# Sixteen pairs of experts behind a transformer block: where the first expert weights are kept, and when the first slot selections are made

## The chip, the cores and the metric

The kernel runs on one core of a Trainium2 chip. The metric is device time in microseconds; three runs of the kernel before took 969.98, 970.21 and 971.9 us, median 970.21. One more execution, the profiled one, took 969.27 us, and its trace spans 967.1 us.

## The reference, cut to what matters

The program computes two blocks over 256 tokens of width 1024, all in float32. The first block is a norm, a recurrence (RG-LRU), sliding-window attention, a feed-forward part and a gated embedding. The second block is latent attention, pooled mixing, cross-attention over a memory of 256 tokens and then a mixture of 32 experts, of which each token takes two. The change concerns the last part:

```python
def hierarchical_moe(xn, w_rg, b_rg, w_re, b_re, w_gate, w_up, w_down):
    ...
    for e in range(N_EXPERTS):
        hid = jax.nn.silu(xn @ w_gate[e]) * (xn @ w_up[e])
        out = out + (hid * cw[..., e:e + 1]) @ w_down[e]
    return out
```

and the memory's cross-attention just before it, `softmax(q k^T) v @ w_o`. An expert has 1024x256 gate and up matrices and a 256x1024 down matrix, so the weights of all 32 experts are about 100 MB, each read once.

## The kernel before, in words

**Units.** All weights come in units of one slot of 128 partitions x 2048 float32 (1 MB), in an order fixed by `plan_units` and numbered i. The dense units, 0 to NUD-1, end with four of w_xo (the output matrix of the memory's attention) and the small router unit. They go to four `raw` slots in turn (NRAW = 4). ScalarE and VectorE split each into a high and a low part (`wh`, `wl`, three pairs, NW = 3; lines 998 and 1548), and TensorE does three products per tile on the parts (lines 472 to 474).

**Experts.** After NUD come 96 expert units for 16 pairs of experts. Pair p has four `moe_in` units (gate and up, two DMAs of 512 KB each) and two `moe_out` units (down, one DMA of 1 MB); `moe_out` of pair p-1 stands behind `moe_in` of pair p. They are not split: TensorE multiplies from the slot itself. They use 15 slots in a ring, `MSLOTS`. So the first 15 units are loaded as soon as their places come free from earlier work, and each later unit is a refill, loaded when the unit 15 places ahead of it has been used (`used`). Refill 1 is the unit numbered 15 after the first, counting from 0, and goes where unit 0 was.

**The queue.** `load(i)` waits on SP for a semaphore and issues the unit's DMAs (line 416). All weight loads are on SP, in program order, so one that waits holds back all behind it. Before the change the ring is `ga, gb, bt`, three raw slots, the six `wh`/`wl` buffers, `s0`, a raw slot, `s1`. The first three units are issued among the w_xo units; the others need a late split or the last uses of `wh` and `wl`.

**The sparse part.** `pe_sparse` (called when no expert has more than 48 tokens) gathers the tokens of eight experts at a time into `XG` (line 2451), and goes through the pairs: `pe_rise(p)` is gate and up (line 2480), then `pe_down(p-1)` (line 2503), then `pe_choose(p+1)`, `pe_turn_hidden(p)`, `pe_spread(p-2)`. `pe_choose(p)` (line 2430) makes the pair's selection and slot weights in a bank of PSUM, which ScalarE copies to `SET` (`act_choose`, line 2568) and VectorE reduces to `CS` (`dve_slot_weights`, line 2634). Its bank is `rise_bank(max(p, 1))`, so selections 0 and 1 both use the bank in which pair 1 rises, and pair p's rise cannot start before both readers are done. Between rise and down the activation is ScalarE's tanh and two VectorE operations on `HS` (lines 2592, 2645, 2648), a transpose on TensorE (`pe_turn_hidden`, line 2488) and a copy to `HT` (line 2608). For pair 0 there is no down of an earlier pair between rise and transpose.

Work buffers `RA`, `RB`, `RC`, `RD`, `KT` belong to attention, recurrence and memory. They and `th`, `tl` are given back before the sparse part, whose own buffers (`XN`, `SEL0`, `XG`, `YY` and others) take the place.

Of the kernel before, what the change touches and what calls it, by code (L numbers as in the profile page):

```python
# [74 lines left out]
def plan_units():  # L75
# [63 lines left out]
    [f"raw_{i}" for i in (*range(NRAW), "ga", "gb", "bt", "s0", "s1", *(f"{x}{n}" for n in range(NW) for x in ("wh", "wl")))] +  # L139
# [21 lines left out]
def build(nc, A, out):  # L161
    with ExitStack() as ctx:
# [24 lines left out]
        BT = sb("BT", 2304)  # L187
        WH = [sbe(f"wh{i}", SLOT, R) for i in range(NW)]
        WL = [sbe(f"wl{i}", SLOT, R) for i in range(NW)]
        RA = sbe("RA", 2080)  # L190
        RB = sbe("RB", 2048)
        RC = sbe("RC", 2048)
        RD = sbe("RD", 1024)
        KT = sbe("KT", 1024)
        TH, TL = [0, 0], [0, 0]
        for i in range(2):
            TH[i], TL[i] = sbe(f"th{i}", 2048, R), sbe(f"tl{i}", 2048, R)
# [32 lines left out]
        FLAT.update({"ga": GA[:, :], "gb": GB[:, :], "bt": BT[:, 0:2048], "s0": S0[:, :], "s1": S1[:, :]})  # L230
        last_w = [i % NW for i in range(NUD - 1 - NW, NUD - 1)]
        MSLOTS = ["ga", "gb", "bt"] + late_slots[:-1] + [f"{x}{n}" for n in last_w for x in ("wh", "wl")] + ["s0"] + late_slots[-1:] + ["s1"]
# [142 lines left out]
        def load(i):  # L375
            _, parts = units[i]
            kc, w = shape_of(i)
            flat = FLAT[slot(i)]
            dst = v3(flat, kc, w)
            m = i - NUD  # L380
            if m >= NM:
                SP.wait_ge(S["used"], i - NM + 1)
            elif m >= NM - 2:
                SP.wait_ge(S["used"], ROUTER + 1)
            elif m == NM - 3:
                SP.wait_ge(S["square"], SQ["w_xo_2"] + 4)
            elif m >= 2 + NRAW:
                SP.wait_ge(S["used"], ROUTER - NW + (m - 2 - NRAW) // 2 + 1)
            elif m in (0, 1, 2):
                SP.wait_ge(S["turn_mm"], TB_["m2"] + 8)  # L390
            elif i >= NRAW:
                before = NUD - NRAW + m - 3 if m >= 3 else i - NRAW
                if before == 0:
                    SP.wait_ge(S["used"], 1)
                else:
                    SP.wait_ge(S["lo"], before)
# [25 lines left out]
        def sp_main():  # L422
# [26 lines left out]
            for i in range(NUD + 3, NUD + NM):  # L449
                load(i)  # L450
# [285 lines left out]
        def pe_main():  # L736
# [233 lines left out]
            for t in range(2):  # L970
                m = PE.matmul(PB[b1][:, 36 * t:36 * t + 36], KT[0:100, 128 * t:128 * t + 128], cst("fold", 36)[0:100, :], start=(t == 0),
# [182 lines left out]
        def act_main():  # L1154
# [353 lines left out]
            ACTE.activation(KT[0:100, 0:256], PB[banks_of(("router", 0))[0]][0:100, 0:256], ACT.Copy).then_inc(S["logits"], 1)  # L1508
# [13 lines left out]
        def pool_main():  # L1522
# [6 lines left out]
            POOL.wait_ge(S["xs_mm"], 4)  # L1529
            POOL.wait_ge(S["xv_mm"], 4)  # L1530
# [856 lines left out]
        def sparse(late):  # L2387
# [68 lines left out]
            def pe_rise(p):  # L2456
# [4 lines left out]
                for r in range(4):  # L2461
# [71 lines left out]
            def pe_sparse():  # L2533
# [10 lines left out]
                for p in range(NP + 1):  # L2544
# [4 lines left out]
                    if p + 1 < NP:  # L2549
# [8 lines left out]
                    if p == 0:  # L2558
                        pe_turn_hidden(0)
# [18 lines left out]
            def act_sparse():  # L2578
# [7 lines left out]
                act_choose(0)  # L2586
                for p in range(NP + 1):
                    if p < NP:
# [13 lines left out]
                    if p + 1 < NP:  # L2602
# [33 lines left out]
            def dve_sparse():  # L2636
                dve_split_weights()
                dve_slot_weights(0)
                for p in range(NP + 1):
# [14 lines left out]
                    if p + 1 < NP:  # L2654
# [206 lines left out]
        FLAT.update({f"{x}{n}": sb(f"m{x}{n}", SLOT)[:, :] for x in ("wh", "wl") for n in range(NW)})  # L2861
# [41 lines left out]
```

## Time and profile before

| | |
|---|---|
| median of three runs | 970.21 us |
| profiled execution | 969.27 us |
| its span | 967.1 us |
| TensorE busy | 951.4 us, 98% |
| VectorE, ScalarE busy | 534.3 us, 469.7 us |
| first gather to last expert matmul | about 724 to 956 us |
| granted TensorE clock, mean | 0.997 |

How to read it: matmuls are pipelined and their ends are modelled, so that two in a row overlap by a little, and the start of the next row tells the pace. A row of the timeline that merges several instructions gives the start of the first and the time over all. A DMA row gives the median time from issue on SP to landing; asked for a narrow stretch it is that of one DMA. Idle time in brackets is that of the engine just before the row, with what ended it.

### The profile page before, as it was taken

The page shows a single profiled execution, that of the slowest core. Times are in us where ns is not written, and L with a number is a line of the kernel's source. Part 1 is how long each engine was busy: PE and PEld are TensorE (multiplying, and loading weights), DVE is VectorE, ACT ScalarE, POOL GpSimd, SP SyncE. Part 2 cuts the span into 40 slices and gives each one's busy share as a digit, 9 for nine tenths or more (in the row PEclk, how much of TensorE's full clock was granted, in tenths as well). Part 3 has the DMA queues.
Part 4 walks back from the last instruction along what each step waited for, and adds up shares of the span by engine and source line. Part 5 has one row for each costly group of instructions (what it writes and reads, how often), then busy time and mean ns, then how long its engine had stood idle before and what let it go on. Part 6 is the DMA issues. An engine that isn't in the chain of part 4 may idle for free.

```text
span 967.1 us, 13220 instructions
## 1 busy us (share of the span) xinstructions
PE 951.4 (98%) x5313; PEld 723.6 (75%) x5313; DVE 534.3 (55%) x848; ACT 469.7 (49%) x733; POOL 2.5 (0%) x12
## 2 busy tenths in 40 slices
PE   9999999999999999999999999999999999999996
PEld 8879887887889889989889887889874354544442
DVE  5888896675666555554586875676453212122123
ACT  5588655756444444444566756445452131211213
POOL 0000000000000000000000000000000000000000
PEclk9999999999999999999999999999999999999998
DMA  9935565424456545554645735365389999999994
GB/s 319 305 132 175 174 218 175 168 94 175 144 183 198 194 175 175 175 179 153 204 146 178 237 113 168 137 238 198 93 323 379 396 393 394 394 393 394 393 394 168
DMA packets 107265, 223.48 MB, mean 231 GB/s; under 512 B 10185, under 2 KB 15042, under 8 KB 107202
## 3 DMA queue, kind: packets, MB, share of 16 engines
q1 hardware_dynamic: 104752, 219.10, 63.7%
q10 hardware_dynamic: 2450, 3.51, 1.1%
q8 instruction: 44, 0.72, 0.3%
q14 instruction: 19, 0.16, 0.0%
HBM read 221.54 MB, written 1.05 MB: 230 GB/s over the span
## 4 chain that ended last, share of the span: by engine, by line
PE 96%; DVE 2%; ACT 1%; issue 1%; DMA 1%; ACTq 0%; DVEq 0%
PE pb L472 21%; PE pb L474 21%; PE pb L473 21%; PE pb L2480 12%; PE pb L2503 6%; PE pb L2518 3%; PE pb L2451 2%; PE pb L562 2%; PE pb L633 1%; PE pb L645 1%; PE pb L582 1%; PE pb L709 1%; PE pb L732 1%; PE pb L536 1%; PE pb L2430 1%
## 5 line engine op out<-in xcount | busy, mean ns | idle before, releaser
L1548 DVE TENSOR_TENSOR wl<-raw,wh 128x2048 fp32r<-128x2048 f32 (+3 forms) x112 | 246.4, 2208 | 96.6 <-ACT wh L998 96.4
L998 ACT ACTIVATE wh<-raw 128x2048 fp32r<-128x2048 f32 (+3 forms) x112 | 206.1, 1847 | 111.5 <-PE pb L474 102.2
L472 PE MATMUL pb<-wh,th 128*128 128x512 f32 (+2 forms) x620 | 247.8, 400 | 0.0
L474 PE MATMUL pb<-wh,tl 128*128 128x512 f32 (+2 forms) x620 | 241.5, 390 | 0.0
L473 PE MATMUL pb<-wl,th 128*128 128x512 f32 (+2 forms) x620 | 241.3, 389 | 0.0
L472 PE MATMUL pb<-th,wh 128*128 128x256 f32 x528 | 152.0, 288 | 0.0
L474 PE MATMUL pb<-th,wl 128*128 128x256 f32 x528 | 149.0, 282 | 0.0
L473 PE MATMUL pb<-tl,wh 128*128 128x256 f32 x528 | 148.7, 282 | 0.0
L472 PEld LDWEIGHTS pb<-wh,th 128*128 128x128 f32 x620 | 116.7, 188 | 27.0 <-issue 4.1
L474 PEld LDWEIGHTS pb<-wh,tl 128*128 128x128 f32 x620 | 116.7, 188 | 25.4
L473 PEld LDWEIGHTS pb<-wl,th 128*128 128x128 f32 x620 | 116.9, 189 | 22.6
L472 PEld LDWEIGHTS pb<-th,wh 128*128 128x128 f32 x528 | 99.6, 189 | 3.2 <-issue 2.7
L473 PEld LDWEIGHTS pb<-tl,wh 128*128 128x128 f32 x528 | 99.6, 189 | 0.5
L474 PEld LDWEIGHTS pb<-th,wl 128*128 128x128 f32 x528 | 99.4, 188 | 0.0
L2645 DVE SCALAR_TENSOR_TENSOR HS<-HS,pb 128x256 f32<-128x256 f32 x16 | 6.7, 422 | 141.5 <-ACT HS L2592 141.5
L2592 ACT ACTIVATE HS<-pb 128x256 f32<-128x256 f32 x16 | 6.1, 384 | 120.9 <-PE pb L2480 120.9
L2653 DVE TENSOR_TENSOR YL<-pb,YH 128x512 fp32r<-128x512 f32 x32 | 22.1, 692 | 34.7 <-ACT YH L2601 34.7
L2601 ACT ACTIVATE YH<-pb 128x512 fp32r<-128x512 f32 x32 | 19.1, 597 | 39.6 <-PE pb L2503 39.6
L2480 PE MATMUL pb<-raw,XG 128*64 128x512 f32 x152 | 35.2, 596 | 0.0
L1014 ACT ACTIVATE th<-pb,PC 128x256 fp32r<-128x256 f32 x45 | 18.8, 479 | 27.3 <-PE pb L562 27.3
L2480 PEld LDWEIGHTS pb<-raw,XG 128*64 128x64 f32 x152 | 10.7, 137 | 20.0 <-issue 20.0
L2518 PE MATMUL pb<-YH,SET 128*128 128x512 f32 x60 | 24.9, 415 | 0.0
(396 smaller groups left out, 1071.3 us busy)
## 6 DMA issues: line engine op xcount, KB each, us to landing
raw<-in_w_in SPq DMA_DIRECT2D x31, 1024.0 KB, 5.1
raw<-in_w_up SPq DMA_DIRECT2D x16, 1024.0 KB, 5.6
raw<-in_w_down SPq DMA_DIRECT2D x16, 1024.0 KB, 4.8
raw<-in_w_exp_gate SPq DMA_DIRECT2D x19, 512.0 KB, 11.8
raw<-in_w_exp_up SPq DMA_DIRECT2D x19, 512.0 KB, 11.7
raw<-in_w_xkv SPq DMA_DIRECT2D x8, 1024.0 KB, 5.0
raw<-in_w_exp_down SPq DMA_DIRECT2D x8, 1024.0 KB, 13.9
mwh<-in_w_exp_gate SPq DMA_DIRECT2D x12, 512.0 KB, 11.7
```

The costliest lines, as they stand in the source:

```text
L472: PE.matmul(o, lh, rh, start=start, stop=False, skip_group_check=True)
L473: PE.matmul(o, lh, rl, start=False, stop=False, skip_group_check=True)
L474: return PE.matmul(o, ll, rh, start=False, stop=stop, skip_group_check=True)
L562: m = PE.transpose(PB[b][:, 128 * t:128 * t + 128], x, ident)
L998: ACTE.activation(hi_of(i), raw_of(i), ACT.Copy).then_inc(S["hi"], 1)
L1548: DVE.tensor_tensor(lo_of(i), raw_of(i), hi_of(i).bitcast(F), ALU.subtract).then_inc(S["lo"], 1)
L2451: m = PE.matmul(b[:, 0:384].rearrange("p (e n) -> p e n", e=SET_E), XN4[i][:, t, k], slots_of(SEL0, t), start=(t == 0 and i == 0), stop=(t ...
L2480: m = PE.matmul(b[64 * j:64 * j + 64, :].rearrange("p (g n) -> p g n", g=2), XG[:, c + CAP * j:c + CAP * j + 64], w[:, :, j, k], start=(kk ...
L2503: m = PE.matmul(PB[6 + h][64 * j:64 * j + 64, :], HT[p % 2][:, 128 * k + 64 * j:128 * k + 64 * j + 64], w[:, j, 512 * h:512 * h + 512], st ...
L2518: m = PE.matmul(PB[2 * t + h][:, :], SET[p % 4][:, 128 * t:128 * t + 128], YY[p % 2][i][:, 512 * h:512 * h + 512], start=(p == 0 and i == ...
L2601: ACTE.activation(YY[(p - 1) % 2][0][:, 512 * h:512 * h + 512], PB[6 + h][:, :], ACT.Copy).then_inc(S["yy_hi"], 1)
L2653: DVE.tensor_tensor(lo, PB[6 + h][:, :], hi.bitcast(F), ALU.subtract).then_inc(S["yy_lo"], 1)
```

## The change

The ring still has 15 slots, but other ones. `RA`, `RB`, `RC` and the joined `RD` and `KT` (`RDK`) are now permanent and serve as slots, `th0` and `tl0` too, and the six `wh`/`wl` buffers no longer do; the sparse part's buffers lie in their place. Each slot has a wait of its own. The router's copy goes to `ROW` instead of `KT`, and the clearing of `SEL0` waits for the last w_xo unit. In the sparse part, selections 1 and 2 move into the rises of pairs 0 and 1, ahead of their fourth unit, and the transpose of pair 0 moves behind the first unit of pair 1.

```diff
-        MSLOTS = ["ga", "gb", "bt"] + late_slots[:-1] + [f"{x}{n}" for n in last_w for x in ("wh", "wl")] + ["s0"] + late_slots[-1:] + ["s1"]
+        MSLOTS = ["rd", "ga", "gb", "bt", late_slots[0], "th", "tl", "ra", "rc", late_slots[1], "rb", late_slots[2], "s0", late_slots[3], "s1"]
...
             if m >= NM:
                 SP.wait_ge(S["used"], i - NM + 1)
-            elif m >= NM - 2:
+            elif m >= 0 and slot(i) == "rd":
+                SP.wait_ge(S["used"], U["gates2", 3, 1] + 1)
+            elif m >= 0 and slot(i) in ("ga", "gb", "bt"):
+                SP.wait_ge(S["turn_mm"], TB_["m2"] + 8)
+            elif m >= 0 and slot(i) in ("th", "tl"):
+                SP.wait_ge(S["used"], U["w_xq_2", 1, 1] + 1)
+            elif m >= 0 and slot(i) in ("ra", "rc"):
+                SP.wait_ge(S["xs_mm"], 4)
+            elif m >= 0 and slot(i) == "rb":
+                SP.wait_ge(S["xv_mm"], 4)
+            elif m >= 0 and slot(i) == "s0":
+                SP.wait_ge(S["square"], SQ["w_xo_2"] + 4)
+            elif m >= 0 and slot(i) in ("s1", late_slots[3]):
                 SP.wait_ge(S["used"], ROUTER + 1)
...
                 if i == U["w_xo_2", 0, 0]:
-                    for m in range(3):
+                    for m in range(4):
                         load(NUD + m)
...
-            POOL.wait_ge(S["xs_mm"], 4)
-            POOL.wait_ge(S["xv_mm"], 4)
+            POOL.wait_ge(S["used"], ROUTER)
             POOL.memset(SEL0[:, :].bitcast(F).rearrange("p (a n) -> p a n", n=64)[:, :, CAP:64], 0.0).then_inc(S["zero"], 1)
...
                     elif p == 0 and r == 2:
                         pe_choose(0)
+                    elif p == 1 and r == 1:
+                        pe_turn_hidden(0)
+                    if p < 2 and r == 3:
+                        pe_choose(p + 1)
...
-                    if p + 1 < NP:
+                    if 2 <= p < NP - 1:
                         pe_choose(p + 1)
...
-                    if p == 0:
-                        pe_turn_hidden(0)
```

`act_sparse` and `dve_sparse` take the copies and reductions of selections 1 and 2 in the same new order.

On TensorE, from the third unit of pair 0 to the first unit of pair 2. `IW,SEL` is a selection, `XG` a rise, `CT,HS` a transpose, `HT` a down. Before:

```order
L2480 MATMUL pb<-BT,XG 64x512 x4
L2480 MATMUL pb<-raw,XG 64x512 x4
L2430 MATMUL pb<-IW,SEL 128x256 x2
L2488 MATMUL pb<-CT,HS 128x128 x2
L2480 MATMUL pb<-raw,XG 64x512 x8
L2480 MATMUL pb<-mwh,XG 64x512 x4
L2480 MATMUL pb<-mwl,XG 64x512 x4
L2503 MATMUL pb<-mwh,HT 64x512 x4
L2503 MATMUL pb<-mwl,HT 64x512 x4
L2430 MATMUL pb<-IW,SEL 128x256 x2
L2488 MATMUL pb<-CT,HS 128x128 x2
L2480 MATMUL pb<-mwh,XG 64x512 x4
```

And the same place in the changed kernel:

```order
L2488 MATMUL pb<-GB,XG 64x512 x4
L2434 MATMUL pb<-IW,SEL 128x256 x2
L2488 MATMUL pb<-BT,XG 64x512 x4
L2488 MATMUL pb<-raw,XG 64x512 x4
L2496 MATMUL pb<-CT,HS 128x128 x2
L2488 MATMUL pb<-mth,XG 64x512 x4
L2488 MATMUL pb<-mtl,XG 64x512 x4
L2434 MATMUL pb<-IW,SEL 128x256 x2
L2488 MATMUL pb<-RA,XG 64x512 x4
L2511 MATMUL pb<-RC,HT 64x512 x4
L2511 MATMUL pb<-raw,HT 64x512 x4
L2496 MATMUL pb<-CT,HS 128x128 x2
```

A unit of rise now stands between each selection and the rise that needs its bank, and one between the end of pair 0's rise and its transpose. Nothing is added or dropped. The next row in the changed kernel is the first unit of pair 2.

On SP, the loads behind the router's. Before, from the third of the three raw slots on:

```order
L416 DMA raw<-in_w_exp_gate 128x2x512
L416 DMA raw<-in_w_exp_up 128x2x512
L416 DMA mwh<-in_w_exp_gate 128x2x512
L416 DMA mwh<-in_w_exp_up 128x2x512
L416 DMA mwl<-in_w_exp_gate 128x2x512
L416 DMA mwl<-in_w_exp_up 128x2x512
L416 DMA mwh<-in_w_exp_down 128x2x1024
L416 DMA mwl<-in_w_exp_down 128x2x1024
```

Now, from the router's on:

```order
L421 DMA raw<-in_w_router_expert 128x8x32
L421 DMA raw<-in_w_exp_gate 128x2x512
L421 DMA raw<-in_w_exp_up 128x2x512
L421 DMA mth<-in_w_exp_gate 128x2x512
L421 DMA mth<-in_w_exp_up 128x2x512
L421 DMA mtl<-in_w_exp_gate 128x2x512
L421 DMA mtl<-in_w_exp_up 128x2x512
L421 DMA RA<-in_w_exp_gate 128x2x512
L421 DMA RA<-in_w_exp_up 128x2x512
L421 DMA RC<-in_w_exp_down 128x2x1024
L421 DMA raw<-in_w_exp_down 128x2x1024
```

Two units of operand space (`mth`, `mtl` are `th0`, `tl0`) and two of attention's work space now stand between the first raw slot and the second, where the six split buffers (`mwh`, `mwl`) stood behind the third. `RB` follows the last row shown.

## Rows read from the trace of the kernel before

**Rows 1.** Page, parts 1 and 2: busy time by engine, GB/s in 40 slices.

```profile
PE 951.4 (98%) x5313; PEld 723.6 (75%) x5313; DVE 534.3 (55%) x848; ACT 469.7 (49%) x733; POOL 2.5 (0%) x12
...
GB/s 319 305 132 175 174 218 175 168 94 175 144 183 198 194 175 175 175 179 153 204 146 178 237 113 168 137 238 198 93 323 379 396 393 394 394 393 394 393 394 168
```

**Rows 2.** TensorE's waits from 700 us on: in total, times, longest us.

```profile
PE pb L2480 <- ACT SET L2568: 1.2, 1, 1.2
PE pb L2488 <- DVE HS L2648: 1.0, 1, 1.0
```

**Rows 3.** Timeline of TensorE: start, us, line, tiles, count, idle before.

```profile
738.16 0.50 PE L2430 MATMUL pb<-IW,SEL 128*128 128x256 f32 x2
739.69 0.44 PE L2488 MATMUL pb<-CT,HS 128*128 128x128 f32 x2 [1.02 <-DVE HS L2648]
740.14 3.65 PE L2480 MATMUL pb<-raw,XG 128*64 128x512 f32 x16
...
752.48 1.94 PE L2480 MATMUL pb<-mwh,XG 128*64 128x512 f32 x8 [1.17 <-ACT SET L2568]
...
925.04 1.94 PE L2480 MATMUL pb<-mwl,XG 128*64 128x512 f32 x8
...
938.01 1.94 PE L2480 MATMUL pb<-raw,XG 128*64 128x512 f32 x8
```

**Rows 4.** Timeline of SP's issues, the last first loads and some refills.

```profile
720.92 1.23 SPq L416 DMA_DIRECT2D S<-in_w_exp_down  x1
730.08 0.37 SPq L416 DMA_DIRECT2D GA<-in_w_exp_down  x1
...
734.67 0.47 SPq L416 DMA_DIRECT2D GB<-in_w_exp_up  x1
...
745.54 0.37 SPq L416 DMA_DIRECT2D mwh<-in_w_exp_down  x1
...
932.67 3.74 SPq L416 DMA_DIRECT2D raw<-in_w_exp_down  x3
```

**Rows 5.** DMA issues in narrow stretches (720, 730, 735, 745, 932 us): KB, us to landing.

```profile
S<-in_w_exp_down SPq DMA_DIRECT2D x1, 1024.0 KB, 14.0
...
GA<-in_w_exp_down SPq DMA_DIRECT2D x1, 1024.0 KB, 7.4
...
GB<-in_w_exp_up SPq DMA_DIRECT2D x1, 512.0 KB, 5.5
...
mwh<-in_w_exp_down SPq DMA_DIRECT2D x1, 1024.0 KB, 8.9
...
raw<-in_w_exp_down SPq DMA_DIRECT2D x1, 1024.0 KB, 13.9
```

**Rows 6.** Timeline of the weight loads on TensorE, the last wait for a DMA.

```profile
946.58 0.21 PEld L2503 LDWEIGHTS pb<-raw,HT 128*64 128x64 f32 x4 [0.65 <-DMA raw<-in_w_exp_down]
```

**Rows 7.** DMA issues on an idle queue: w_xkv, page part 6; a pair at 693.8 us.

```profile
raw<-in_w_xkv SPq DMA_DIRECT2D x8, 1024.0 KB, 5.0
...
raw<-in_w_exp_up SPq DMA_DIRECT2D x1, 512.0 KB, 4.9
```

**Rows 8.** Stretches: length, busy PE, PEld, DVE, ACT, POOL, PEclk, DMA share, GB/s.

```profile
740.00:750.00 10.00, 9.98 (x48) 4.03 (x48) 0.90 (x2) 0.93 (x3) 0.00 (x0) 1.00 1.02 373
760.00:780.00 20.00, 20.00 (x96) 9.83 (x93) 6.04 (x14) 4.51 (x11) 0.00 (x0) 1.00 1.04 393
```

**Rows 9.** Timeline of ScalarE and VectorE around the first selection and activation.

```profile
734.69 0.38 ACT L2568 ACTIVATE SET<-pb 128x256 fp32r<-128x256 f32 x1 [1.72 <-PE pb L2430]
735.10 0.35 DVE L2634 TENSOR_REDUCE CS<-pb 64x1 f32<-64x2 f32 x2 [3.05 <-ACT SET L2568]
738.28 0.38 ACT L2592 ACTIVATE HS<-pb 128x256 f32<-128x256 f32 x1 [3.21 <-PE pb L2480]
```

**Rows 10.** The w_xo loads: SP's issues, one's landing (651 to 653 us), a split on ScalarE.

```profile
652.27 10.35 SPq L416 DMA_DIRECT2D raw<-in_w_xo  x3
...
raw<-in_w_xo SPq DMA_DIRECT2D x1, 1024.0 KB, 8.0
...
671.48 1.91 ACT L998 ACTIVATE wh<-raw 128x2048 fp32r<-128x2048 f32 x1
```

More of the change, by code:

```diff
@@ L138 @@
 SEMAPHORES = (
-    [f"raw_{i}" for i in (*range(NRAW), "ga", "gb", "bt", "s0", "s1", *(f"{x}{n}" for n in range(NW) for x in ("wh", "wl")))] +
+    [f"raw_{i}" for i in (*range(NRAW), "rd", "ga", "gb", "bt", "th", "tl", "ra", "rc", "rb", "s0", "s1")] +
     ["d_x", "d_rows", "d_first", "d_const", "d_bd", "d_bcast", "d_mem", "d_mem1", "d_pos", "d_gffn", "d_poolw", "d_p", "d_fing",
@@ L187, in build @@
         BT = sb("BT", 2304)
+        RA = sb("RA", 2080)
+        RB = sb("RB", 2048)
+        RC = sb("RC", 2048)
+        RDK = sb("RDK", 2048)
+        RD, KT = RDK[:, 0:1024], RDK[:, 1024:2048]
+        TH, TL = [sbe("th0", 2048, R), 0], [sbe("tl0", 2048, R), 0]
         WH = [sbe(f"wh{i}", SLOT, R) for i in range(NW)]
         WL = [sbe(f"wl{i}", SLOT, R) for i in range(NW)]
[L190 to L197, printed above, removed]
+        TH[1], TL[1] = sbe("th1", 2048, R), sbe("tl1", 2048, R)
         BD = BT[:, 0:1024]
@@ L229, in build @@
         FLAT = {n: RAW[n][:, :] for n in range(NRAW)}
-        FLAT.update({"ga": GA[:, :], "gb": GB[:, :], "bt": BT[:, 0:2048], "s0": S0[:, :], "s1": S1[:, :]})
-        last_w = [i % NW for i in range(NUD - 1 - NW, NUD - 1)]
-        MSLOTS = ["ga", "gb", "bt"] + late_slots[:-1] + [f"{x}{n}" for n in last_w for x in ("wh", "wl")] + ["s0"] + late_slots[-1:] + ["s1"]
+        FLAT.update({"rd": RDK[:, :], "ga": GA[:, :], "gb": GB[:, :], "bt": BT[:, 0:2048], "ra": RA[:, 0:2048], "rc": RC[:, :], "rb": RB[:, :], "s0": S0[:, :], "s1": S1[:, :]})
+        MSLOTS = ["rd", "ga", "gb", "bt", late_slots[0], "th", "tl", "ra", "rc", late_slots[1], "rb", late_slots[2], "s0", late_slots[3], "s1"]
         NM = len(MSLOTS)
@@ L382, in load @@
                 SP.wait_ge(S["used"], i - NM + 1)
-            elif m >= NM - 2:
-                SP.wait_ge(S["used"], ROUTER + 1)
[L385 to L390, printed above, removed]
+            elif m >= 0 and slot(i) == "rd":
[11 more added lines that the diff above has]
+            elif m >= 0 and slot(i) in ("s1", late_slots[3]):
+                SP.wait_ge(S["used"], ROUTER + 1)
+            elif m >= 0:
+                SP.wait_ge(S["lo"], NUD - NRAW + late_slots.index(slot(i)))
             elif i >= NRAW:
-                before = NUD - NRAW + m - 3 if m >= 3 else i - NRAW
-                if before == 0:
+                if i == NRAW:
                     SP.wait_ge(S["used"], 1)
                 else:
-                    SP.wait_ge(S["lo"], before)
+                    SP.wait_ge(S["lo"], i - NRAW)
             for (name, lead, r0, n, c0, cw, at) in parts:
@@ L446, in sp_main @@
                 if i == U["w_xo_2", 0, 0]:
-                    for m in range(3):
+                    for m in range(4):
                         load(NUD + m)
-            for i in range(NUD + 3, NUD + NM):
+            for i in range(NUD + 4, NUD + NM):
                 load(i)
@@ L970, in pe_main @@
             for t in range(2):
-                m = PE.matmul(PB[b1][:, 36 * t:36 * t + 36], KT[0:100, 128 * t:128 * t + 128], cst("fold", 36)[0:100, :], start=(t == 0),
+                m = PE.matmul(PB[b1][:, 36 * t:36 * t + 36], ROW[0:100, 128 * t:128 * t + 128], cst("fold", 36)[0:100, :], start=(t == 0),
                               stop=True, skip_group_check=True)
@@ L1507, in act_main @@
             act_done(("router", 0), 0)
-            ACTE.activation(KT[0:100, 0:256], PB[banks_of(("router", 0))[0]][0:100, 0:256], ACT.Copy).then_inc(S["logits"], 1)
+            ACTE.activation(ROW[0:100, 0:256], PB[banks_of(("router", 0))[0]][0:100, 0:256], ACT.Copy).then_inc(S["logits"], 1)
             ACTE.activation(unused, eps, ACT.Exp).then_inc(S["root"], 1)
@@ L2586, in act_sparse @@
                 act_choose(0)
+                act_choose(1)
                 for p in range(NP + 1):
+                    if p == 1:
+                        act_choose(2)
                     if p < NP:
@@ L2860, in build @@
         early.close()
-        FLAT.update({f"{x}{n}": sb(f"m{x}{n}", SLOT)[:, :] for x in ("wh", "wl") for n in range(NW)})
+        FLAT.update({"th": sb("mth", 2048)[:, :], "tl": sb("mtl", 2048)[:, :]})
         normed = ExitStack()
```

7 lines of the change are left out of this document (5 added, 2 removed).

## Prediction

> **What bounds the kernel now.** I read four views in this order. The page first: TensorE is busy 951.4 of 967.1 us, and from the thirtieth slice on (a slice is 24.2 us) the DMA queues move 379 to 396 GB/s without a pause [rows 1]. So in the experts' part two resources look full at once. The question is which of them ends the kernel.
>
> TensorE's waits come second. From 700 us on, two waits of more than half a microsecond stand in the list, 1.2 us for the copy of a selection and 1.0 us for the activation of pair 0 [rows 2], both at the start, before pair 2 [rows 3]. After that TensorE goes at a fixed pace: pair 14 begins at 925.04 us and pair 15 at 938.01, so 12.97 us for a pair's six units, 2.16 us a unit [rows 3].
>
> The DMA side comes third, from issues and landings. Refill 1 is issued at 730.08 us and lands 7.4 us later, at 737.5. Refill 2 lands at 734.67 + 5.5 = 740.2, refill 7 at 745.54 + 8.9 = 754.4, and refill 79 at 932.67 + 13.9 = 946.6 [rows 4, 5]. Between refills 2 and 7 that is 14.2 / 5 = 2.85 us a unit, between 7 and 79 it is 192.2 / 72 = 2.67 us a unit, which is 1.049 MB at 393 GB/s [rows 8].
>
> So TensorE is the faster of the two by half a microsecond a unit. It lives on the 15 units loaded ahead, and the lead is used up just at the end: at 946.58 us TensorE waits 0.65 us for refill 79, the second down unit of pair 14, the only wait for a DMA in this part [rows 6]. The balance is nearly exact. A gain on TensorE alone is eaten by that wait, and the end then follows the landing of refill 79.
>
> **The change part by part.** I cost each part against the profiled execution, 969.27 us, which is 0.94 us below the median of 970.21 us. The difference that comes out is put on the median.
>
> *The transposes behind the first unit of pair 1, selection 1 in the rise.* Before, selection 1 starts at 738.16 us, the transpose waits until 739.69 and pair 1 begins at 740.14 [rows 3]. A selection followed by a rise takes about 0.43 us, so pair 1 could have begun at 738.6, 1.55 us sooner. The transposes come back between its first two units and take the 0.45 us that they took. The net is 1.1 us, about the 1.0 us that the list of waits has. The cover is one unit of rise, 3.65 / 2 = 1.8 us or 1.72 us of pace. It must hide two things. First, selection 0 to its last reader: copy from 734.69, reductions to 735.10 + 0.35 = 735.45, against a selection that started at about 734.15, so 1.3 us; it fits. Second, tanh to transpose: 738.28 to 739.69 is 1.4 us [rows 3, 9], plus some 0.2 us before the tanh; it fits by 0.1 us. If it does not fit, the loss is that tenth or two.
>
> *Selection 2 in the rise of pair 1.* It takes away the 1.17 us before 752.48 [rows 3]. It now waits for `HT` of pair 0, which is ready two units earlier. Both together give TensorE 2.2 us, or 2.3 by the timeline.
>
> *TensorE's bound.* If no DMA held it, the end would come earlier by 2.2 us and by the 0.65 us wait of rows 6, that is 2.9 us.
>
> *First loads earlier.* There are 15 slots before and after. Before, the last first load is issued at 720.92 us and lands at 734.9 [rows 4, 5], so when refill 1 is issued at 730.08, earlier units still land for another 4.8 us. After, four units are issued among the w_xo units, `th` and `tl` when the last w_xq unit is used, `RA` and `RC` after the memory's scores, `RB` after its values; only the last three (`s0`, a raw slot, `s1`) wait for the end of w_xo or the router. I expect all to have landed by about 724 us, and the queue to be idle until 730. It is not asked for anything then: a refill needs a used unit, and the first unit is used at 730.08 as before, because the gathers and the router ahead of it do not depend on these loads. That is the main point. What the early loads can win is only what stands in front of the refills at 730, not their five or ten units.
>
> *Where the refills land.* Refill 1 then takes the 5.0 us of a unit alone and lands at 735.1. Refill 2 is a pair of DMAs; alone, the second lands 4.9 us after its issue [rows 7], so at 734.67 + 4.9 = 739.6, against 740.2. The head start of 2.4 us at refill 1 has shrunk to 0.6 us at refill 2, since between the two stand the gathers, and nothing can be loaded while they run. From refill 2 on, units are asked for faster than they land. At 2.67 us a unit refill 7 lands at 752.9, 1.5 us earlier than before; at 2.85, the pace that these very refills had, it lands at 753.8, 0.6 us earlier. The ends are 0.6 and 1.5. Nothing excludes that a queue with nothing ahead does a little worse still, so I put the lower end at zero. I take 0.6, since the same units in the same order at nearly the same times are the nearest row. From refill 7 on the pace is 2.67 in both kernels.
>
> A page of the Trainium skill prices this otherwise: DMA: Bandwidth & Descriptors, section Anatomy of one DMA, gives about 2.0 us plus bytes over 436 GB/s for one DMA, on its software path. By an estimate from that page refill 2's second DMA would land 3.2 us after its issue, at 737.9, and the gain would be 2.3 us instead of 0.6. The rows have 4.9 us for such a DMA on an idle queue, so the measurement decides and the sum does not use it.
>
> *The end.* TensorE reaches refill 79 at 946.0 - 2.2 = 943.7 us; it lands at 946.6 - 0.6 = 946.0. TensorE waits there 2.3 us or so, and everything behind follows 0.6 us earlier than before.
>
> *At nothing.* The fourth unit among the w_xo loads is 2.7 us more in front of the second w_xo unit, issued at 652.27 us and landed 8.0 us later, at 660.3. The splits have other units to do first: that unit's is not before 671.48 [rows 10], so 8 us are left to cover it. One unit more on SP costs it under 1 us of issuing, long before anything waits. The clearing of `SEL0` moves to the end of w_xo, some 18 us ahead of selection 0, its only reader that waits for it. The router's copy has the same size in another buffer. The sparse part's buffers in the split weights' place are written after the router, when the last split pair is used.
>
> The sum: 0.6 us less, 968.7 us for an execution like the profiled one and **969.6 us** for the median.
>
> **The rivals.**
>
> *A: the tail of loads doesn't bind, TensorE's gain counts in full.* For it: the wait in the list before is only 0.65 us, the idle queue at 724 to 730 us may serve the first refills better than I take, and fewer loads beside the router may help a little. Against: refill 79 would have to land 2.9 us earlier, which no pace seen gives, even 2.67 us from refill 2 on gives 1.5. It gives 970.2 - 2.9 = 967.3 us. The Trainium skill, on the same page in its section Rules for kernel authors, says to issue a DMA early and wait on it late; taken by itself that speaks for A, and the trace limits it by the time at which refills can be issued.
>
> *B: slower, by shallow refills.* The queue starts at 730 us with nothing in it and not, as before, with up to 4.8 us of work. In the first stretch of refills it moved 373 GB/s against 393 later [rows 8]. If refills go at 2.85 us until the queue is deep, and depth takes longer to build because nothing stood ahead, each such unit costs 0.18 us. It starts with 1.5 us to spend, so it decides beyond 8 units, and is a measurable loss beyond (1.5 + 1.9) / 0.18 = 19 units. With 30 it costs 3.9 us, so 974 us. Against it: the queue gains 0.5 us of depth a unit from TensorE's faster pace, and refill 7 already waits 8.9 us.
>
> *C: the new selections wait.* If ScalarE's or VectorE's readers of selection 0 or 1 are late by more than the unit that covers them, TensorE stops where it did not. The price is under 1 us, and the refills' landing still sets the end: 970.2 us, no change.
>
> **How the numbers follow.** A difference of 0.2%, 1.9 us, is about what a measurement of this kernel can tell from no change. My forecast, an end set by the refills and 0 to 1.5 us earlier, has 0.78. A has 0.11, B 0.08, C 0.03. A is the only case that is faster by over 1.9 us, B the only one that is slower. So faster is 0.11, same 0.81, slower 0.08. The range: the forecast's own ends are 968.7 and 970.2, the runs shown lie up to 1.7 us above their median, and the lower end reaches to A. That is 967.3 to 971.2.
>
> **What would show it.** Right: the two waits of rows 2 gone; pair 2 begins at about 750.2 us instead of 752.48; the queue without bytes between about 724 and 731 us; refill 1 landing at 735, refill 2 at 739.6, and refill 79 within 1.5 us of 946.0; TensorE waiting 2 us or more in total for `in_w_exp_down` or its neighbours near the end. It would be wrong if pair 0's first unit were used much before or after 730.08 us, if the DMA rate between 760 and 940 us were other than 393 GB/s, or if TensorE showed a new wait in the dense part between 640 and 714 us. A shows in refill 79 landing before 944 us, B in refill 7 landing after 755 us and the queue below 380 GB/s beyond 780 us.

## Result and profile after

| | before | after |
|---|---|---|
| median of the runs, us | 970.67 (969.98 to 971.9, 4 runs) | 964.57 (963.91 to 964.85, 4 runs) |
| ratio | 1 | 0.9935, interval 0.9918 to 0.9952 |
| profiled execution, us; its span | 969.27; 967.1 | 964.85; 963.0 |

(The row of before has a fourth run, 971.13 us, beside the three of the section on the metric.) The change makes the kernel 6.1 us faster where 0.6 was forecast, and 964.57 us lies below the range of 967.3 to 971.2. The profiled execution of before is shorter than all four of its runs, that of after is the longest of its four, so the two profiles show 4.4 of the 6.1.

The page of the changed kernel, busy time and bytes:

```profile
PE 947.5 (98%) x5313; PEld 722.7 (75%) x5313; DVE 534.4 (55%) x848; ACT 470.1 (49%) x733; POOL 2.5 (0%) x12
...
GB/s 314 303 143 173 155 238 179 156 107 163 152 189 190 204 175 175 175 181 156 202 150 175 246 104 175 131 259 223 290 205 286 393 394 393 394 393 395 393 396 157
```

Against [rows 1] TensorE does the same 5313 instructions in 3.9 us less, and slices 32 to 39, the steady refills, have the same rate as before, 393 to 396 GB/s. So the gain is TensorE's own time, and it isn't in the refills. The timeline of TensorE, the changed kernel (start, us, line, tiles, count):

```profile
723.61 1.94 PE L2488 MATMUL pb<-RDK,XG 128*64 128x512 f32 x8
...
731.95 0.50 PE L2434 MATMUL pb<-IW,SEL 128*128 128x256 f32 x2
...
734.15 1.89 PE L2488 MATMUL pb<-raw,XG 128*64 128x512 f32 x8
735.97 0.44 PE L2496 MATMUL pb<-CT,HS 128*128 128x128 f32 x2
...
746.02 1.94 PE L2488 MATMUL pb<-RB,XG 128*64 128x512 f32 x8
```

and the same first unit before:

```profile
728.10 1.94 PE L2480 MATMUL pb<-GA,XG 128*64 128x512 f32 x8
```

The first expert unit starts at 723.61 instead of 728.10 us, 4.5 us earlier. Pair 2 starts 22.4 us behind it, where it was 24.4, so TensorE does gain its 2.0 us in the first pairs. But from the first expert unit to the end of the span it is 963.0 - 723.6 = 239.4 us, and before 967.1 - 728.1 = 239.0: the experts' part, where all that was meant happens, gained nothing. TensorE's waits and the weight loads that waited, changed kernel:

```profile
PE pb L2511 <- DMA GB<-in_w_exp_down: 0.6, 1, 0.6
PE pb L2511 <- DMA BT<-in_w_exp_down: 0.6, 1, 0.6
...
PE pb L2488 <- DMA GA<-in_w_exp_up: 0.3, 1, 0.3
```

```profile
937.38 0.20 PEld L2488 LDWEIGHTS pb<-GA,XG 128*64 128x64 f32 x4 [1.22 <-DMA GA<-in_w_exp_up]
939.94 0.20 PEld L2511 LDWEIGHTS pb<-GB,HT 128*64 128x64 f32 x4 [1.50 <-DMA GB<-in_w_exp_down]
942.50 0.20 PEld L2511 LDWEIGHTS pb<-BT,HT 128*64 128x64 f32 x4 [1.50 <-DMA BT<-in_w_exp_down]
```

The two waits of [rows 2] are gone and three waits for refills stand near the end, as forecast. The list puts them at 1.5 us in total. The starts tell more: the three units above start 2.56 us apart each, where a unit's pace is 1.72.

So the 4.5 us come from the dense part, where the same work is done in the same order. Weights that are loaded on the way show how they grow: the w_attn_proj unit is issued 0.1 us earlier than before, w_mix_out 3.1 and w_xo 4.0 us. SP's issues, after and then before:

```profile
203.26 0.37 SPq L421 DMA_DIRECT2D raw<-in_w_attn_proj  x1
...
590.21 0.37 SPq L421 DMA_DIRECT2D raw<-in_w_mix_out  x1
...
639.68 0.37 SPq L421 DMA_DIRECT2D raw<-in_w_xo  x1
```

```profile
203.36 0.37 SPq L416 DMA_DIRECT2D raw<-in_w_attn_proj  x1
...
593.34 0.37 SPq L416 DMA_DIRECT2D raw<-in_w_mix_out  x1
...
643.64 0.37 SPq L416 DMA_DIRECT2D raw<-in_w_xo  x1
```

None of TensorE's waits in the dense part went; its products follow each other more closely. In one run of products over split weights, fifteen in a row without a gap, after and then before:

```profile
616.68 0.39 PE L477 MATMUL pb<-wh,th 128*128 128x512 f32 x1
...
619.85 0.39 PE L479 MATMUL pb<-wh,tl 128*128 128x512 f32 x1
```

```profile
619.67 0.39 PE L472 MATMUL pb<-wh,th 128*128 128x512 f32 x1
...
622.92 0.39 PE L474 MATMUL pb<-wh,tl 128*128 128x512 f32 x1
```

Fourteen steps take 3.17 us after, 0.226 a product, and 3.25 before, 0.232. There are 3 x 576 products of this width. Grouped by line and form (busy us, mean ns of one), after and then before:

```profile
L478 PE MATMUL pb<-wl,th 128*128 128x512 f32 x576 | 224.7, 390 | 0.0
...
L478 PE MATMUL pb<-tl,wh 128*128 128x256 f32 x528 | 149.4, 283 | 0.0
```

```profile
L473 PE MATMUL pb<-wl,th 128*128 128x512 f32 x576 | 227.1, 394 | 0.0
...
L473 PE MATMUL pb<-tl,wh 128*128 128x256 f32 x528 | 148.7, 282 | 0.0
```

A product is shown from its start to its modelled end and overlaps the next, so I compare the **pace**: the mean step from one start to the next in a run of products, over the whole trace. With 512 columns, where the split weights move through the array, it is 232.5 ns before and 227.9 after. With 256, where the operands `th` and `tl` move, it is 120.4 and 121.2. That is 1728 x 4.6 = 7.9 us less and 1584 x 0.8 = 1.3 us more. Of these 6.6 us some are lost and 4.5 arrive. A part of the loss can be seen: the weight loads of the first of the three products wait longer for VectorE's part of the split, `wl`. In us and times, before (line 472) and then after (line 477):

```profile
  DVE wl L1548: 0.4, 2
```

```profile
  DVE wl L1552: 2.2, 6
```

The products, their data and their clock are the same: the granted clock of the profiled execution is 0.998 after, and 0.997 to 0.998 in the kernels below. What differs is where the buffers lie. Counted from the program's allocations, in bytes of a partition, with the rest over 256 in brackets:

| | before | after |
|---|---|---|
| `wh0`, `wl0`, ... | 112672 (32), 137248 (32) | 161952 (160), 186528 (160) |
| `th0` | 194720 (160) | 145568 (160) |
| `th1` | 211104 (160) | 211104 (160) |

Of the work buffers only `RA` isn't a multiple of 256 bytes long; its 8320 bytes are 128 more. Before, it lies between the split weights (`wh`, `wl`) and the operands (`th`, `tl`), after, ahead of both. So the distance from the split weights to the operands, over 256, was 128 and is 0. "Distance" below means this rest, split weights minus operands. The count puts the first buffer, `raw0`, at 16512 bytes, which no view shows. The distances don't depend on it; the places themselves, of the slots too, do.

### The profile page after: what moved, and what is told of

Same layout as the page of the kernel before. It is cut to its first block, busy times and chain, and to the rows that moved or that the text cites. A ratio compares the mean times of both kernels' runs of the same rounds, so it can differ in the third digit from the quotient of the medians.

```text
span 963.0 us, 13218 instructions
## 1 busy us (share of the span) xinstructions
PE 947.5 (98%) x5313; PEld 722.7 (75%) x5313; DVE 534.4 (55%) x848; ACT 470.1 (49%) x733; POOL 2.5 (0%) x12
## 3 DMA queue, kind: packets, MB, share of 16 engines
HBM read 221.54 MB, written 1.05 MB: 231 GB/s over the span
## 4 chain that ended last, share of the span: by engine, by line
PE 83%; DVE 7%; ACT 4%; issue 3%; DMA 2%; SPq 1%; POOL 0%; ACTq 0%; DVEq 0%; POOLq 0%
PE pb L477 17%; PE pb L479 17%; PE pb L478 17%; PE pb L2488 11%; PE pb L2511 5%; PE pb L2526 3%; PE pb L2455 2%; DVE wl L1552 2%; ACT wh L1003 2%; PE pb L567 2%; DMA BT<-in_w_exp_down 1%; PE pb L638 1%; DMA raw<-in_w_in 1%; PE pb L650 1%; PE pb L714 1%
## 5 line engine op out<-in xcount | busy, mean ns | idle before, releaser
L479 PE MATMUL pb<-wh,tl 128*128 128x512 f32 (+2 forms) x620 | 239.0, 385 | 0.0
L478 PE MATMUL pb<-wl,th 128*128 128x512 f32 (+2 forms) x620 | 238.8, 385 | 0.0
## 6 DMA issues: line engine op xcount, KB each, us to landing
raw<-in_w_exp_gate SPq DMA_DIRECT2D x18, 512.0 KB, 11.2
S<-in_w_exp_down SPq DMA_DIRECT2D x6, 1024.0 KB, 13.5
```

The lines of the kernel that those rows point to most:

```text
L478: PE.matmul(o, lh, rl, start=False, stop=False, skip_group_check=True)
L479: return PE.matmul(o, ll, rh, start=False, stop=stop, skip_group_check=True)
```

## Experiments

**First round: parts of the change.** The theory: the gain is the places of the buffers, by the distance of 128 or 0. The rivals: the early loads bring it (fewer transfers beside the last dense products), or the selections do.

*e1*, the kernel before with one buffer elsewhere: loads, ring and selections stay.

```diff
+        RA = sbe("RA", 2080)
         WH = [sbe(f"wh{i}", SLOT, R) for i in range(NW)]
         WL = [sbe(f"wl{i}", SLOT, R) for i in range(NW)]
-        RA = sbe("RA", 2080)
...
+        XNLP = sb("XNL", 2080, R)
...
-        XN = [sbe("XNH", 2048, R, normed), sbe("XNL", 2048, R, normed)]
+        XN = [sbe("XNH", 2048, R, normed), XNLP[:, 0:2048]]
```

(`XNLP` has `RA`'s size and stands in the place that it leaves, so that the sparse part still fits.)

> The kernel before, with nothing moved but the work buffer RA, which now lies ahead of the six split buffers wh and wl instead of behind them. So their addresses in a partition are a multiple of 256 bytes plus 160, as in the changed kernel, instead of plus 32; the operands th and tl stay where they were, order of work and loads too. Theory 1, the dense part got faster because of where the split buffers lie relative to a 256-byte boundary: the 512-column products start every 227 ns instead of 230 to 232, the first gather comes about 4.5 us earlier, and the time is 4 to 6 us lower (965 us). Theory 2, it is the region (the far end of the partition, or the distance to th and tl): no change, within 1 us of before. Theory 3, it is the loads or another part of the change: no change either.

*e2*, the kernel before with the new order of selections and of the first transpose alone:

> The kernel before, with only the new order of the first selections and of pair 0's transpose; ring of slots, loads and addresses as before. My forecast's working: TensorE saves 2.2 us before pair 2, the refills land as before (refill 1 at 737.5 us, refill 7 a few tenths earlier), refill 79 is waited for 2 to 3 us, and the time is 0 to 0.5 us lower. If the tail of loads did not bind: 2.2 to 2.9 us lower. The pace of the dense part stays at 230 to 232 ns.

*e3*, the changed kernel with the distance put back to 128 and nothing else (a column is 4 bytes):

```diff
+        sbe("PADA", 32)
         WH = [sbe(f"wh{i}", SLOT, R) for i in range(NW)]
         WL = [sbe(f"wl{i}", SLOT, R) for i in range(NW)]
+        sbe("PADB", 32)
         TH[1], TL[1] = sbe("th1", 2048, R), sbe("tl1", 2048, R)
```

> The changed kernel, with 128 unused bytes ahead of the split buffers and 128 more ahead of th1, so that wh and wl lie at a multiple of 256 bytes plus 32 again, in the far region, and all th and tl at plus 160. Theory 1 (place relative to a 256-byte boundary): 512-column products at 230 to 232 ns again, the time 4 to 6 us above the changed kernel, 969 to 970.5 us. Theory 2 (region or distance): still 227 ns and 964.6 us. Theory 3 (loads or another part): still 964.6 us.

*e4*, the changed kernel with the order of selections of before (the hunks of `pe_sparse`, `act_choose` and `dve_slot_weights` undone):

> The changed kernel, with the first selections and pair 0's transpose put back to the old order; new ring, loads and addresses stay. Theory 1 and 2: the dense part keeps its 227 ns, so 964.6 us plus what the selections are worth. By my working of the end (refills decide) that is 0 to 0.5 us, as TensorE's own 2.2 us only lengthen its waits near the end: 964.6 to 965.1 us. If TensorE decides: 966.8 us.

Measured, with the start of the first expert unit in the profiled execution:

| kernel | us, median (range, runs) | ratio | pace 512, 256 | first expert unit |
|---|---|---|---|---|
| e1 | 965.16 (964.86 to 965.93, 5) | 0.994, 0.9927 to 0.9953 | 227.9, 121.3 | 723.99 |
| e2 | 971.22 (970.41 to 972.71, 11) | 1.0005, 0.9996 to 1.0013 | 232.4, 120.4 | 728.94 |
| e3 | 971.01 (969.51 to 971.81, 11) | 0.9999, 0.999 to 1.0008 | 232.4, 120.4 | 728.50 |
| e4 | 964.74 (963.85 to 966.91, 6) | 0.9941, 0.9929 to 0.9954 | 227.8, 121.2 | 722.49 |

This settles it from both sides. One buffer moved (and `XNL` put in the place it left) gives the kernel before the whole gain (e1), and 256 bytes of padding take it all from the changed kernel, whose early loads and new selections remain (e3). Both rivals fall. The start of the first expert unit says the same. One execution differs from the next, but the two groups stay apart: 728.10 to 728.94 us in the four profiles with distance 128 (before, e2, e3, e5), 722.49 to 724.42 in the eight with distance 0 (the changed kernel, e1, e4, and e7, e10, e11, c1, c2 below).

The selections are worth nothing (e2 against before, e4 against the changed kernel). TensorE's waits say why. In e4 both of [rows 2] are back; in e2, where they are gone, refills are waited for instead:

```profile
PE pb L2484 <- ACT SET L2572: 1.2, 1, 1.2
PE pb L2492 <- DVE HS L2652: 1.0, 1, 1.0
```

```profile
PE pb L2484 <- DMA GB<-in_w_exp_up: 0.8, 1, 0.8
PE pb L2507 <- DMA BT<-in_w_exp_down: 0.6, 1, 0.6
PE pb L2507 <- DMA raw<-in_w_exp_down: 0.6, 1, 0.6
```

1.2 + 1.0 us against 0.8 + 0.6 + 0.6: forecast step by step, and confirmed. What the early loads give is read from kernels that differ in nothing else but the places, at the same distance and with the same selections: e1 and e4, 965.16 and 964.74, or e2 and e3, 971.22 and 971.01. That is 0.4 and 0.2 us, less than the intervals can tell from nothing.

**Second round: distance or place.** If the distance decides, moving everything alike changes nothing.

*e5*, the kernel before, `sb("PADA", 32)` ahead of `WH`: split weights at 160, operands at 32, distance 128 as before.

> The kernel before, with 128 unused bytes ahead of wh0, so that everything behind moves up: wh and wl now lie at a multiple of 256 bytes plus 160, and th and tl at plus 32 (before: 32 and 160). Theory 1a, what counts is that wh and wl have the same place as th and tl relative to 256 bytes (160 and 160 in the changed kernel): here they are 128 apart as before, so 230 to 232 ns and 971 us. Theory 1b, what counts is the place of wh and wl alone, or of the moving operand (wh and wl in the 512-column products): 227 ns and 965 us for the 512-column products; the 256-column ones, whose moving operand is th, may change with th.

*e10*, the changed kernel, `sb("PADA", 32)` ahead of `th0`: all at 32, distance 0.

> The changed kernel, with 128 unused bytes ahead of th0: wh, wl, th and tl all lie at a multiple of 256 bytes plus 32. Theory 1a (same place): 227 ns and 964.6 us, as the changed kernel. Theory 1b (plus 160 for wh and wl itself is what is fast): 232 ns and 970 to 971 us.

*e7*, the same with `sb("PADA", 24)`: all at 0.

> The changed kernel, with 96 unused bytes ahead of th0: wh, wl, th and tl all at a multiple of 256 bytes. Theory 1a: 227 ns, 964.6 us. Theory 1b leaves it open. If starting on a boundary is worth something in itself, the 256-column products fall below 120 ns and the time below 964 us.

*e11*, the changed kernel with 256 bytes where e3 has 128 (`PADA` and `PADB` of 64 columns): distance 0 over 256, another one over 512.

> The changed kernel, with 256 unused bytes ahead of wh0 and 256 more ahead of th1: all of wh, wl, th and tl keep plus 160 relative to 256 bytes, but wh and wl lie 256 bytes off th and tl relative to 512 and to any larger power of two up to 2048. If 256 bytes are the measure: 227 ns and 964.6 us, as the changed kernel. If it is a larger one (512, 1024 or 2048): 232 ns and 970 to 971 us.

*e8* and *e9*, the changed kernel with `PADA`, `PADB` of 24 and 40, and of 16 and 48 columns: distance 96 and 64.

> The changed kernel, with 96 unused bytes ahead of wh0 and 160 ahead of th1: wh and wl at a multiple of 256 bytes, th and tl at plus 160, so 96 apart (160 the other way round). Theory 1a in its strict form: any distance other than 0 is slow, 232 ns and 970 to 971 us. If only a distance of 128 is slow: 227 ns and 964.6 us. Something between would speak for a dependence by degrees.

> The changed kernel, with 64 unused bytes ahead of wh0 and 192 ahead of th1: wh and wl at a multiple of 256 bytes plus 224, th and tl at plus 160, so 64 apart. Theory 1a in its strict form (any distance within 256 bytes is slow, as 96 and 128 were): 232 ns and 970 to 971 us. If only the place within 64 bytes counts: 227 ns and 964.6 us.

*c1* and *c2* are the changed kernel and e7 once more, as controls.

> The changed kernel once more, beside the kernel at plus 0, to compare them on one chip. All theories: 964.6 us, 227 ns.

> The kernel with wh, wl, th and tl at a multiple of 256 bytes once more. It had 963.2 us with the same 227 ns as the changed kernel at 964.6. If that difference is real: 1 to 1.5 us below the changed kernel again. If it was the chip or chance: within 0.5 us of it.

**Third round: other distances, and the slots.** *e15* (48 and 16 columns) has distance 192, *e16* (8 and 56) has 32.

> The changed kernel with wh and wl at a multiple of 256 bytes plus 96, th and tl at plus 160, so wh lies 192 above or 64 below th. If the pace goes by how far apart the two are, in either direction: as 64 apart, 116.8 and 229.5 ns, 962 to 963 us. If it goes by the direction too: other paces, up to the 120 and 232.5 ns of 128 apart with 971 us.

> The changed kernel with wh and wl at plus 192, th and tl at plus 160, so 32 apart. Distances 0, 64, 96, 128 had 227.9, 229.5, 233.4, 232.5 ns for the 512-column products and 121.2, 116.8, 119.6, 120.4 for the 256-column ones. If the pace changes smoothly between 0 and 64: 228 to 229 and 118 to 119 ns, about 963.5 us. If being 32 off a multiple of 64 costs by itself (as 96 seems to): 232 ns or more, 968 to 971 us.

| distance | kernels | pace 512, 256 | by the two paces, us | us, median (range, runs) | first expert unit |
|---|---|---|---|---|---|
| 128 | e5 | 232.5, 120.6 | +0.3 | 971.02 (969.62 to 972.19, 11) | 728.40 |
| 0 | e10 | 227.9, 121.3 | -6.5 | 965.03 (964.55 to 966.44, 5) | 724.42 |
| 0 | e11 | 227.8, 121.2 | -6.9 | 964.67 (964.24 to 965.83, 5) | 722.85 |
| 0 | c1 | 227.9, 121.2 | -6.7 | 964.69 (963.71 to 964.91, 5) | 722.92 |
| 0 | e7 | 227.9, 121.3 | -6.5 | 963.22 (962.87 to 963.73, 5) | 722.68 |
| 0 | c2 | 227.9, 121.2 | -6.7 | 963.21 (962.24 to 963.61, 5) | 723.05 |
| 64 | e9 | 229.5, 116.8 | -10.9 | 962.34 (960.25 to 962.77, 5) | 719.72 |
| 96 | e8 | 233.4, 119.6 | +0.3 | 970.26 (969.73 to 971.81, 11) | 728.28 |
| 192 | e15 | 233.3, 119.2 | -0.5 | 969.95 (969.08 to 971.89, 11) | 728.06 |
| 32 | e16 | 233.2, 119.7 | +0.1 | 970.18 (969.63 to 971.16, 11; one more took 2057.25) | 728.86 |

The fourth column is 1728 times the step of the one pace from before plus 1584 times that of the other. It parts the kernels into the same three groups as the first expert unit (near 728, 723 and 720 us), though not in the same order within a group. Of the saving in that column between 57% (e10) and 83% (e7) arrive there. The distance decides, not the place (e5, e10), and at distance 0 another 256 bytes change nothing (e11). It is not symmetric: 64 above is the best, 192, which is 64 below, is as bad as 128. The two widths don't agree on the best distance either. I had expected one smooth rule or one favoured place; both fell, and no cause inside TensorE or SBUF is shown here. ScalarE and VectorE write the next splits while TensorE multiplies, and no run takes them out, so it isn't shown either that TensorE's two reads alone make the difference.

In e9 the first expert unit starts 3.2 us earlier than in the changed kernel beside it (c1), but the median is only 2.35 us lower: TensorE waits for refills four times near the end, 2.4 us in the list, where c1 has three waits and 2.0:

```profile
PE pb L2490 <- DMA GA<-in_w_exp_up: 0.8, 1, 0.8
PE pb L2513 <- DMA GB<-in_w_exp_down: 0.6, 1, 0.6
PE pb L2513 <- DMA BT<-in_w_exp_down: 0.6, 1, 0.6
...
PE pb L2513 <- DMA S<-in_w_exp_down: 0.4, 1, 0.4
```

**The slots.** e7 and c2 beat c1 by 1.5 us at the same pace, and their gain stands behind the first expert unit (238.4 us from there to the end of the span in both; in the other kernels above it is 239.3 to 240.7, and before 239.0). Their DMA rate is 397 GB/s. Stretch 760 to 930 us, the changed kernel and then e7:

```profile
760.00:930.00 170.00, 170.00 (x808) 78.45 (x805) 31.34 (x74) 39.10 (x83) 0.00 (x0) 1.00 1.04 394
```

```profile
760.00:930.00 170.00, 170.00 (x807) 78.90 (x803) 32.16 (x76) 39.51 (x84) 0.00 (x0) 1.00 1.04 397
```

In e7 two of the 15 slots, `th0` and `tl0`, begin on a multiple of 256 bytes. The question was whether 64 bytes would do. (By the count of places above, 6 slots of the changed kernel and 8 of e7 lie on 64 bytes, not 8 and 10 as the expectation of e13 has it; the test is the same.) *e13* puts every slot on a multiple of 64 (`sb("PADG", 8)` ahead of `GA`); *e14* is e13 with distance 64 (and `PADA` 16, `PADB` 48).

> The changed kernel, with 32 unused bytes ahead of GA. Everything behind moves up by 32 bytes: wh, wl, th and tl stay at the same place relative to each other (all plus 192), and all 15 slots of the expert ring now start on a multiple of 64 bytes, where 8 of 15 did in the changed kernel and 10 of 15 in the kernel with the operands at plus 0. Theory S, the transfers are faster into slots on 64 bytes (397 GB/s between 760 and 930 us with 10 of 15, 394 with 8): about 405 GB/s with all 15, a pace of 227 ns as before, the experts' part shorter by 2 to 4 us until TensorE decides, so 961 to 963 us. Theory T, the 397 GB/s came from something else in that kernel (starting at a multiple of 256): 394 GB/s and 964.6 us.

> The same, with 64 more unused bytes ahead of wh0 and 192 ahead of th1: slots on 64 bytes, and wh and wl 64 bytes off th and tl, as in the run that had 962.3 us. Theory S: both gains add, about 116.8 ns for the 256-column products and 229.5 ns for the 512-column ones, the first rise at about 720 us, and 958 to 960.5 us in all. Theory T: 962.3 us. If the pace goes by the absolute place and not by the distance, the 256-column pace is back at 120 ns.

e13: 965.05 us (964.59 to 965.88, 5 runs), 394 GB/s, so 64 bytes do nothing. e14: 961.70 (961.2 to 962.05, 4 runs), by its distance: 3.35 us below e13, with 393 GB/s and the paces of e9, 229.5 and 116.8 ns, at other places (split weights at 0, operands at 192). Then all 15 slots on multiples of 256, with distance 0 in *e18* and 64 in *e17*, both made from the changed kernel:

```diff
+        sb("PADR", 32)
         RAW = [sb(f"raw{i}", SLOT) for i in range(NRAW)]
...
+        sb("PADG", 24)
         GA = sb("GA", 2048)
...
         RA = sb("RA", 2080)
+        sb("PADB0", 32)
         RB = sb("RB", 2048)
...
+        sbe("PADA", 16)
         WH = [sbe(f"wh{i}", SLOT, R) for i in range(NW)]
         WL = [sbe(f"wl{i}", SLOT, R) for i in range(NW)]
+        sbe("PADB", 48)
         TH[1], TL[1] = sbe("th1", 2048, R), sbe("tl1", 2048, R)
```

(e18 has the first three added lines alone. The lines shown are those around each edit.)

> The changed kernel with unused bytes at three places (128 ahead of the raw slots, 96 ahead of GA, 128 behind RA), so that all 15 slots of the expert ring, and wh, wl, th and tl with them, start on a multiple of 256 bytes. Slots on 64 bytes had no effect (394 GB/s, 965.1 us), two of 15 on 256 had 397 GB/s and 963.2 us, twice. Theory T, each slot on 256 bytes is faster to fill: 15 of 15 give well over 400 GB/s between 760 and 930 us, no wait of TensorE for a DMA is left, the experts' part is 2 to 3 us shorter than in the changed kernel and TensorE decides, 961 to 962.5 us; the pace stays at 227.9 and 121.2 ns. Theory U, it was something particular to the two slots th0 and tl0, or to th and tl at plus 0: 397 GB/s and 963.2 us as in that run.

> The same, with wh and wl 64 bytes off th and tl. Theory T: the first rise at about 719.5 us, no waits for DMAs, 116.8 and 229.5 ns, and the gains of both add: 957 to 959.5 us, the fastest of all. Theory U: 960 to 961 us. If the refills cannot keep up with a first rise 4 us earlier even at their better rate, some waits for exp_down stay and the time is between.

e18: 961.57 us (961.22 to 962.01, 4 runs), ratio 0.99, interval 0.9883 to 0.9916. e17: **957.75** us (956.18 to 958.68, 4 runs), ratio 0.9858, interval 0.9841 to 0.9876. Their rate is 411 GB/s in both, and the paces are those of their distance to within 0.3 ns. The stretch of e17, and its waits from 700 us on, all of them:

```profile
760.00:930.00 170.00, 170.00 (x806) 79.03 (x804) 32.15 (x76) 39.55 (x84) 0.00 (x0) 1.00 1.04 411
```

```profile
PE pb L981 <- ACT ROW L1518: 0.5, 1, 0.5
PE pb L2553 <- DVE SEL L1936: 0.4, 1, 0.4
PE pb L994 <- DVE MK L1993: 0.2, 1, 0.2
```

411 GB/s instead of 394 and no wait for a refill is left: TensorE now decides to the end, 237.1 us from its first expert unit in both. So the distance now counts in full: e17's first expert unit starts at 719.06 us and e18's at 722.90, 3.8 us apart, and so are the medians. e17 beats both kernels, before by 13.5 us (971.29 beside it) and the changed one by 6.8.

## Why the prediction was wrong

**The step that failed** is the last of the sum, "At nothing". It priced the new places of the buffers ("The sparse part's buffers in the split weights' place") by one question, whether they are written after their last reader. What the move did to the buffers that stay was not asked: `th`/`tl` and `wh`/`wl` changed their distance from 128 to 0, and 3312 dense products changed their pace, worth 6.0 us by e1 against before and 6.4 by e3 against the changed kernel. Out of this came the second wrong statement, that pair 0's first unit is used at 730.08 us "as before", because the gathers and the router do not depend on the loads. They don't; but the dense part ended 4.5 us sooner, and that unit was used at 725.59 us. No row of before could give a price, since the profile has no addresses and only one layout. An unpriced term with both ends open should have widened the range; the text named the sign itself ("wrong if pair 0's first unit were used much before or after 730.08") without giving it a chance. All three rivals lie in the experts' part, where the change was aimed.

**The change without the new distance** is e3: 971.01 us against 971.12 for before beside it. That is 0.1 us, inside the forecast's own 0 to 1.5, but the 0.6 can't be told from nothing by it.

**TensorE's gain**, 2.2 us before pair 2: right, 2.0 us. The selection in the rise costs nothing, and its copy, reductions and the transpose don't wait: C did not happen.

**An end set by the refills**: right. e2 shows it without the change of pace: TensorE's 2.2 us turn into 2.0 us of waits. The forecast had 2.3 us near the end; the changed kernel has 1.5 us in the list, and by the starts more, as said above. TensorE's bound, 2.9 us, can be read in e18, where no refill holds it: 237.05 us for the experts' part against 239.03 is 2.0. That is the gain before pair 2 and nothing else. The other term, the 0.65 us of [rows 6], was worth nothing: it is a wait of the weight load, and the products of that unit start 1.72 us behind those of the unit before, at TensorE's pace. Before:

```profile
944.92 1.89 PE L2503 MATMUL pb<-BT,HT 128*64 128x512 f32 x8
946.64 1.89 PE L2503 MATMUL pb<-raw,HT 128*64 128x512 f32 x8
```

Where a weight load waits, look at the products behind it before the wait is put into a sum. The loads that start earlier don't bring A about; a higher rate does.

**The queue and the refills.** The forecast puts them by the clock; I take them from the first expert unit on, 723.61 and 728.10 us. SP's issues of refills 1, 2 and 7, changed kernel:

```profile
725.59 0.37 SPq L421 DMA_DIRECT2D RDK<-in_w_exp_down  x1
...
730.17 0.47 SPq L421 DMA_DIRECT2D GA<-in_w_exp_up  x1
...
740.03 0.37 SPq L421 DMA_DIRECT2D mtl<-in_w_exp_down  x1
```

and their way to landing, in us:

```profile
RDK<-in_w_exp_down SPq DMA_DIRECT2D x1, 1024.0 KB, 4.9
...
GA<-in_w_exp_up SPq DMA_DIRECT2D x1, 512.0 KB, 4.6
...
mtl<-in_w_exp_down SPq DMA_DIRECT2D x1, 1024.0 KB, 10.4
```

They land at 730.5, 734.8 and 750.4 us. From the first unit on that is 6.9, 11.2 and 26.8 us, and before 9.4, 12.1 and 26.3 [rows 4, 5]. The queue was idle, as told, but for 2.8 us and not 6: the last first load, issued at 713.77 us, landed 9.0 later, at 722.8, less than a microsecond ahead of the first unit:

```profile
713.77 0.47 SPq L421 DMA_DIRECT2D S<-in_w_exp_down  x1
```

```profile
S<-in_w_exp_down SPq DMA_DIRECT2D x1, 1024.0 KB, 9.0
```

```profile
724.00:726.00 2.00, 2.00 (x11) 0.81 (x8) 1.86 (x10) 0.72 (x2) 0.00 (x0) 1.00 0.03 8
```

(the last is the stretch from 724 to 726 us, with 8 GB/s). Refill 1 comes 2.5 us sooner (forecast 2.4), refill 2 0.9 sooner (forecast 0.6). But refill 7 comes 0.5 us later where 0.6 sooner was put: 3.1 us a unit between 2 and 7, not 2.85. Nor is the head start there at the end: the weights of refill 79 are taken at 942.50 us, 218.9 us behind the first unit, and before at 946.58, 218.5 behind it [rows 6]. The rates of 4 us:

```profile
736.00:738.00 2.00, 2.00 (x12) 0.80 (x12) 0.00 (x0) 0.38 (x1) 0.00 (x0) 1.00 1.05 347
738.00:740.00 2.00, 2.00 (x11) 0.52 (x7) 0.00 (x0) 0.00 (x0) 0.00 (x0) 1.00 0.99 271
```

The DMA engines are busy all the time (share 1.05 and 0.99) and move less, and this took back the 0.6 us. B as a whole fell, with 394 GB/s from 760 us on. Nor is it shown that the dip is B's mechanism, the empty queue: between 12 and 18 us behind the first unit the rate is 373 GB/s before, 324 in the changed kernel, 358 in e4 (new loads alone) and 331 in e2, which has the new selections alone and the queue of before. So both parts lower it. Why, no run tells.

## What to carry to other kernels

When a change moves buffers, list the addresses of everything that stays, before and after, and ask of each pair of operands and each DMA destination how it lies over 256 bytes, and run a second layout: a side effect of the layout can outweigh all that the change is about. When a large change gives a gain, first find the stage in which it arises (here, the start of one fixed instruction before and after), and then undo the layout alone with a few bytes of padding. Where two resources are balanced, as here, try both together: the last 6.8 us came from padding alone, and 64 bytes of distance gave 3.8 us with the other limit gone (e18 to e17), and 2.35 and 3.35 without (c1 to e9, e13 to e14).

## What the runs showed of the hardware

- In this kernel the pace of back-to-back products of 128x128 tiles depends on where the weights and the moving operand lie against each other over 256 bytes: 227.8 to 233.4 ns with 512 columns, 116.8 to 121.3 ns with 256. Distances of 0, 32, 64, 96, 128 and 192 bytes were run, and the mechanism stays open.
- A weight load can wait without holding a product: 0.65 us before refill 79 in the kernel before, with the products at their pace of 1.72 us a unit.
- The rate of loads from HBM rose with the start of their slots: 394 GB/s with none of 15 on a multiple of 256 bytes, 397 with two, 411 with all, and 393 to 394 with all on a multiple of 64. The Trainium skill, DMA: Bandwidth & Descriptors, section How a descriptor splits into AXI transactions, says that a descriptor that starts off a 256-byte boundary costs extra beats. It says so of bytes that are fetched, while here the side that is written moved. The trace agrees in the direction, for the side in SBUF: over the same stretch a packet of 2 KB takes 88.3 ns on the mean in e13 and 84.2 in e17. That it is the same rule isn't shown.
